# Probabilities divided on GpSimd, mixed values kept on chip

## The reference

```
proj = rmsnorm(x) @ w_in
oa = window attention  (8 query heads, 2 key heads, rotary, keys within 128, a sink per head)
ob = neighbourhood attention (8 heads, grid of 64 columns, 8 rows x 16 columns, bias table)
    s = q k * scale (+ bias or mask);  p = exp(s - max);  o = (p / sum p) v
x  = x + concat(rmsnorm(oa, g_out_a), rmsnorm(ob, g_out_b)) @ w_out
h  = rmsnorm(x);  aff = softmax(h @ w_router);  each of 16 experts takes its best tokens
x  = x + sum over experts of gate * SwiGLU(h)
y  = rmsnorm(x, g_final)
```

## Time and profile before

| | us |
|---|---|
| median of 3 runs (2483.33 to 2484.32) | 2483.69 |
| the profiled execution | 2484.71 |
| its span in the profile | 2482.9 |

### The profile page before, as it was taken

How to read it: one execution, slowest core, us unless ns; L and a number is a source line. 1 busy time by engine, 2 the same in 40 slices (tenths; PEclk the granted TensorE clock), 3 DMA queues, 4 the chain that set the end, 5 groups by cost and what they waited for, 6 DMA issues and landing times.

```text
span 2482.9 us, 43086 instructions
## 1 busy us (share of the span) xinstructions
PE 2434.5 (98%) x16395; PEld 2178.7 (88%) x16395; DVE 1673.5 (67%) x2432; ACT 1456.5 (59%) x2050; POOL 163.7 (7%) x172
## 2 busy tenths in 40 slices
PE   9999999999889999999999999999999999999997
PEld 7888877777579989899998989999998989999896
DVE  6355278854776767676666767666676767666677
ACT  4332189977555656556565656555565655656574
POOL 0000000000010101101010100101010110101010
PEclk9999999999989999999999999999999999999998
DMA  7353255354376767767676767767676776767696
GB/s 250 123 177 113 62 163 202 122 186 154 111 286 224 260 224 258 240 241 247 234 248 233 250 234 248 256 230 251 223 259 226 256 244 238 251 230 253 228 325 222
DMA packets 104549, 545.29 MB, mean 220 GB/s; under 512 B 11344, under 2 KB 19920, under 8 KB 54800
## 3 DMA queue, kind: packets, MB, share of 16 engines
q1 hardware_dynamic: 97072, 518.19, 59.6%
q0 software_dynamic: 7392, 25.96, 4.5%
HBM read 503.21 MB, written 40.89 MB: 219 GB/s over the span
## 4 chain that ended last, share of the span: by engine, by line
PE 69%; DVE 1%; DMA 1%; ACT 1%; issue 0%; POOL 0%; SPq 0%; DVEq 0%; ACTq 0%
PE ex_gate_ps L2043 16%; PE ex_up_ps L2043 16%; PE ex_gate_ps L2045 7%; PE ex_up_ps L2045 7%; PE ex_down_ps L2058 2%; PE ex_down_ps L2062 2%; PE ex_down_ps L2059 2%; PE ex_down_ps L2060 2%; PE ex_down_ps L2063 2%; PE ex_up_ps L2058 2%; PE ex_up_ps L2062 2%; PE ex_up_ps L2063 2%; PE ex_up_ps L2060 2%; PE ex_up_ps L2059 2%; DMA fi_x<-acc_scratch 1%; PE ex_turn_ps L2011 0%
## 5 line engine op out<-in xcount | busy, mean ns | idle before, releaser
L1879 DVE TENSOR_TENSOR ex_w_lo<-ex_w,ex_w_hi 128x2048 fp32r<-128x2048 f32 x384 | 879.8, 2292 | 440.5 <-ACT ex_w_hi L1775 437.1
L1775 ACT ACTIVATE ex_w_hi<-ex_w 128x2048 fp32r<-128x2048 f32 x384 | 733.4, 1910 | 208.7 <-PE ex_down_ps L2063 106.8
L2043 PE MATMUL ex_gate_ps<-ex_xt,ex_w_hi 128*128 128x384 f32 x2048 | 591.8, 359 | 0.7 <-DVE ex_xt L1885 0.7
L2043 PE MATMUL ex_up_ps<-ex_xt,ex_w_hi 128*128 128x384 f32 x2048 | 592.1, 359 | 0.0
L2045 PE MATMUL ex_up_ps<-ex_xt,ex_w_lo 128*128 128x192 f32 x2048 | 512.7, 250 | 0.0
L2045 PE MATMUL ex_gate_ps<-ex_xt,ex_w_lo 128*128 128x192 f32 x2048 | 512.7, 250 | 0.0
L2045 PEld LDWEIGHTS ex_gate_ps<-ex_xt,ex_w_lo 128*128 128x128 f32 x2048 | 391.1, 191 | 0.6
L2045 PEld LDWEIGHTS ex_up_ps<-ex_xt,ex_w_lo 128*128 128x128 f32 x2048 | 391.2, 191 | 0.0
L2043 PEld LDWEIGHTS ex_gate_ps<-ex_xt,ex_w_hi 128*128 128x128 f32 x2048 | 384.5, 188 | 1.6 <-issue 1.0
L2043 PEld LDWEIGHTS ex_up_ps<-ex_xt,ex_w_hi 128*128 128x128 f32 x2048 | 384.5, 188 | 0.0
L1797 ACT ACTIVATE ex_up_low<-ex_up_ps 128x384 f32<-128x384 f32 x128 | 62.9, 492 | 207.8 <-PE ex_up_ps L2045 207.8
(11 more groups left out here) (310 smaller groups left out, 4012.3 us busy)
## 6 DMA issues: line engine op xcount, KB each, us to landing
ex_w<-in_w_experts SPq DMA_DIRECT2D x384, 1024.0 KB, 4.8
pj_w<-in_w_in SPq DMA_DIRECT2D x54, 512.0 KB, 3.7
pj_xr<-in_xt SPq DMA_DIRECT2D x12, 512.0 KB, 6.0
o_scratch<-ld_out SPq DMA_DIRECT2D x24, 256.0 KB, 4.6
at_bias<-in_near_bias SPq DMA_DIRECT2D x4, 1536.0 KB, 8.8
q_p<-in_x SPq DMA_DIRECT2D x12, 512.0 KB, 4.5
acc_scratch<-k_p SPq DMA_DIRECT2D x12, 512.0 KB, 5.4
h_scratch<-q_p SPq DMA_DIRECT2D x12, 512.0 KB, 3.0
```

The source lines that it names most:

```text
L1775: act.activation(w_hi[:, c % SLOTS, :], w[:, c % SLOTS, :], ACT.Copy).then_inc(hi_w, 1)
L1879: dve.tensor_tensor(w_lo[:, c % SLOTS, :], w[:, c % SLOTS, :], w_hi[:, c % SLOTS, :].bitcast(F32), ALU.subtract).then_inc(lo_w, 1)
L2043: nc.tensor.matmul(out[:, b, 0:2 * CAP], w_hi[:, slot, f], xt[:, k, :, :].rearrange("p h c -> p (h c)"), start=k == 0, stop=False)
```

## The change

In `attend` the reciprocals are taken one turn earlier (unit u-1), and GpSimd multiplies the probabilities of each head by them in place. The flips, still of unit u-2, wait for GpSimd. Values are weighed for unit u-3, and DVE copies the mixed tile of unit u-4, which is already transposed, over that unit's own queries, `queries(v)`. The two output transposes, ACT's copy for them, the multiplication on DVE and all traffic of `o` are gone. Scores have four banks, probabilities eight slots, the bias two slots, the mixed tile two banks. At the end ACT and DVE prepare the first tile and four slices of `w_out`.

In `mix` tiles are read from the queries by `Mixed.parts`, in three pieces (a 128x512 one, two strided 128x256 ones). Every tile keeps the two head groups apart (A and B) and is scaled when it is added, in two adds of two instructions each. The sums of squares are made from squares on ACT, two folding adds on GpSimd and a matmul against ones (`tally`), two tiles at a time. Rows of `w_out` and `g_out` are reordered to match on the host.

```diff
@@ attend
-        PROBS, STATS, BIASES, V_SLOTS, SCORES = 4, 8, 3, 2 * len(V_TILES), 3
+        PROBS, STATS, BIASES, V_SLOTS, SCORES = 8, 8, 2, 2 * len(V_TILES), 4
-        FLIP, WEIGH, OUT, STEPS = 2, 4, 4, N + 4
+        INVERT, FLIP, WEIGH, OUT = 1, 2, 3, 4
+        STEPS = N + OUT + 1
+        def queries(v, rows):
+            b, pair, _ = units[v]
+            if b.window:
+                return keep.q.at(rows, pair, b.tile * P, P)
+            return keep.q.at(rows, QA + pair, b.kind * GROUP + b.strip * P, P)
...
+                    if not b.window and b.number + BIASES < len(near_start):
+                        sp.wait_ge(added, 2 * PAIRS * (step + 1))
                         load_bias(b.number + BIASES)
...
+        @block.gpsimd
+        def _(pool):
+            for v in range(N):
+                b, r = units[v][0], v % STATS
+                pool.wait_ge(inverted, v + 1)
+                for h in range(2):
+                    p = probs[:, (2 * v + h) % PROBS, 0:b.keys]
+                    pool.tensor_scalar(p, p, rden[:, r, h:h + 1], None, ALU.mult).then_inc(shared_out, 1)
@@ scalar
-                    act.activation(o_turn[:, v % 2, :], mixed_ps[:, 0:P], ACT.Copy).then_inc(o_copied, 1)
...
                 if u == N - 1:
-                    split(0)
+                    act.wait_ge(kept, PAIRS * (FIRST_TILES + 1))
+                    for dst, src in mixed.parts(0, lead.m_hi):
+                        act.activation(dst, src, ACT.Copy).then_inc(lead.hi_m, 1)
+                if N <= u < N + LEAD_SPLITS:
+                    split(u - N)
@@ vector
+                if 0 <= u - OUT < N:
+                    v = u - OUT
+                    dve.wait_ge(weighed, v + 1)
+                    dve.tensor_copy(queries(v, slice(0, P)), mixed_ps[v % 2][:, 0:P]).then_inc(kept, 1)
@@ tensor
-                        pe.wait_ge(exped, 2 * v + h + 1)
+                        pe.wait_ge(shared_out, 2 * v + h + 1)
...
-                    turned = [nc.tensor.transpose(out_ps[:, h, 0:HD], o_turn[ROWS[h], v % 2, :],
-                                                  ident[ROWS[h], ROWS[h]]) for h in range(2)]
@@ mix, gpsimd
+            for t in range(TILES):
+                own = squares[:, t % 2, :, :].rearrange("p (l j) c -> p l j c", l=2)
+                pool.wait_ge(mixed_squared, Mixed.PARTS * (t + 1))
+                pool.tensor_tensor(own[:, :, 0:2, :], own[:, :, 0:2, :], own[:, :, 2:4, :], ALU.add).then_inc(paired, 1)
...
+                pool.tensor_tensor(partial[:, t % (2 * PAIR), :, :], own[:, :, 0, :], own[:, :, 1, :],
+                                   ALU.add).then_inc(folded, 1)
@@ mix, scalar: before the steps, then at the end of each
+            for t in range(2):
+                square_mixed(t)
+            for j in range(LEAD_SPLITS, DT):
                 split(j)
             raise_m(1)
+            take_root1(0)
...
+                if s + 3 < TILES:
+                    square_mixed(s + 3)
@@ mix, vector
+                    dve.scalar_tensor_tensor(out=x2[t % 2][:, c], in0=bank_of(t, part, k)[:],
+                                             scalar=rs1[:, i % 2, col:col + 1],
+                                             in1=(x if part == A else x2)[t % 2][:, c],
+                                             op0=ALU.mult, op1=ALU.add).then_inc(summed, 1)
...
+                add(t, B)
...
+                if s % 2 == 0 and s < TILES:
+                    invert1(s // 2)
...
+                if t < LAST:
+                    scale_h(t)
+                    search(s, 1)
+                    if n < TILES:
+                        lower(n)
+                    add(s, A)
+                dve.wait_ge(routed, t + 1)
@@ mix, tensor
+            def tally(i):
+                pe.wait_ge(folded, PAIR * (i + 1))
+                for t in range(PAIR * i, PAIR * (i + 1)):
+                    for part in (A, B):
+                        col = 2 * (t % PAIR) + part
+                        last = nc.tensor.matmul(ss1[:, col:col + 1], partial[:, t % (2 * PAIR), part, :], ones[:],
+                                                start=True, stop=True)
+                last.then_inc(tallied, 1)
...
-                    if n < TILES:
-                        turn_merged(n)
```

More of the change, by code:

```diff
@@ L114 @@
 class Lead:
[L118 to L123, removed]
-        self.m_hi, self.m_lo = sb("ld_m_hi", [P, DT, P], F32R)[:], sb("ld_m_lo", [P, DT, P], F32R)[:]
[L125 to L135, removed]
+    FIRST_LO, HI = 6, 4
@@ L136, in __init__, with parts @@
         self.w_in = [sem(f"ld_w_in{i}") for i in range(DT)]
-        self.squared, self.root, self.refined = sem("ld_squared"), sem("ld_root"), sem("ld_refined")
-        self.normed, self.turned = sem("ld_normed"), sem("ld_turned")
         self.hi_m, self.lo_m, self.hi_w, self.lo_w = (sem(f"ld_{n}") for n in ("hi_m", "lo_m", "hi_w", "lo_w"))
[L140 to L150, removed]
+class Mixed:
+    PARTS = 1 + 2
+    def __init__(self, q):
+        self.q = q
+    def parts(self, t, dst):
+        rows, tile = slice(0, P), self.q.at(slice(0, P), slice(0, QA), t * P, P)
+        pieces = [(dst[:, 0:QA, :], tile)]
+        g, first = divmod(t, G_TILES)
+        strips = self.q.at(rows, slice(QA, DT), g * GROUP, GROUP).rearrange(
+            "p j (s r c) -> p j s r c", s=STRIPS, r=Q_ROWS)
+        into = dst[:, QA:DT, :].rearrange("p j (r s c) -> p j r s c", r=2, s=STRIPS)
+        return pieces + [(into[:, :, r, :, :], strips[:, :, :, 2 * first + r, :]) for r in range(2)]
@@ new lines, in square_mixed, with take_root1 @@
+            def square_mixed(t):
+                if t >= 2:
+                    act.wait_ge(folded, t - 1)
+                for dst, src in mixed.parts(t, squares[:, t % 2, :, :]):
+                    act.activation(dst, src, ACT.Square).then_inc(mixed_squared, 1)
+            def take_root1(i):
+                act.wait_ge(tallied, i + 1)
+                if i:
+                    act.wait_ge(refined1, REFINE * i)
+                act.activation(rt1[:], ss1, ACT.Sqrt, bias=eps[:], scale=1.0 / HALF).then_inc(root1, 1)
@@ L1407, in _ @@
                     last.then_inc(parted, 1)
-                both(s, range(3, 5))
+                if s < TILES:
+                    project(s, B, pieces[3:5])
+                if s == 0:
+                    pe.wait_ge(ready, 1)
+                    tally(0)
                 if 0 <= t:
@@ L2226, in layouts @@
     a["sink"] = np.broadcast_to(i["sink_a"][0][order], (P, 2 * PAIRS))
-    a["w_out"] = i["w_out"][0].reshape(DT, P, D)
+    mixed = [HD * h + e for h in order for e in range(HD)] + list(range(D // 2, D))
+    a["w_out"] = i["w_out"][0][mixed].reshape(DT, P, D)
     router = i["w_router"][0].reshape(DT, P, EXPERTS).transpose(1, 0, 2)
```

507 lines of the change are left out of this document (198 added, 309 removed).

## The result

The changed kernel takes 2560.68 us (median of 4 runs, 2560.18 to 2562.11) against 2484.01 in the runs beside it: slower by 3.1%, ratio 1.0310, 95% interval 1.0292 to 1.0328. The profiled execution's span went from 2482.9 to 2558.5 us. The forecast was 2474 with a range to 2495.

A forecast was written before the change was run, and what follows sets the result against it. TensorE was taken to set attention's turn (PE busy 185.0 of 185.9 us). Attention -13.3, bias +1.0, seam +0.7, steady steps +0.7 and search steps +0.6 sum to -10.3: 2483.7 to 2473.4, stated as 2474 us, range 2466 to 2495.

The forecast's parts named there:

- step 3: Attention: two bias slots instead of three make a stall for the last block's bias, +1.0 us (0 to 4).
- Step 1: Attention: TensorE loses two output transposes and gets back 0.21 us a turn, 2.08 to 1.87 us at 384 keys.
- Step 2, the ring: Attention: flips wait for GpSimd, which waits for DVE's reciprocal; two turns of 384 keys take 2.45+2X us.
- the price: Attention: X, the time of one GpSimd multiplication, is 0.63 us for 384 columns, between 0.49 and 1.01.
- Step 4: Between attention and mixing: extra copies and splits make the passage 41.4 us against 40.7, +0.7 us (0 to +2.5).
- Step 5: Mixing, steady steps: DVE's half add makes TensorE wait 0.9 us, not 0.42; seven steps, +0.7 us (-3.5 to +2).
- Step 6: Mixing steps under DVE's search: half add and scaled add bring 1.5 us, passing one step by 0.6; +0.6 us.
- A: Attention: GpSimd dearer than a turn can carry, breaking even at 0.83 us an instruction; 2495 to 2504 us; chance 0.22.
- TensorE's clock: Attention: sign of wrong working if the granted clock falls below 1.00 because of TensorE's new waits; no size given.

The follow-up runs named there:

- experiment 5: Changed kernel with GpSimd multiplying only 138 of 384 columns (the forecast's price), the rest left undivided: 2509.19 us, ratio 1.0105.
- experiment 6: Changed kernel with GpSimd multiplying only 138 of 384 columns and the flips three turns behind the scores, not two: 2483.64 us, ratio 0.9998.
- experiment 3: Changed kernel with flips three turns behind the scores, not two, mixing and keeping one turn later, GpSimd's work unchanged: 2514.52 us.
- experiment 9: Kernel before the change with only its two output transposes a turn left out, the output staying unturned: 2479.26 us, ratio 0.9981.
- experiment 12: Changed kernel with GpSimd copying each head's probabilities onto themselves in place of multiplying them: 2495.47 us, ratio 1.0039.
- experiment 10: Changed kernel with GpSimd's multiplication left out altogether, flips waiting for the exponentials: 2483.58 us, ratio 0.9999.
- experiment 7: Changed kernel with DVE's half add in the mixing stage moved behind the routing probabilities: 2561.26 us.

## Why the prediction was wrong, point by point

The forecast's 2474 and the measured 2560.7 differ by 86.7 us, which the runs split: price 51.5 (2560.7 to experiment 5's 2509.2), ring 25.6 (to experiment 6's 2483.6), the rest 9.6. The first two depend on the order in which they are mended: with the ring opened first (experiment 3) the ring is worth 46.2 and the price 30.9. Of the rest 6.9 are attention (in experiment 6 the last exponential came 6.4 us sooner than before, not 13.3) and 3.0 the seam, where the longer pipeline took 3.7 more than before and not 0.7; the bias wait that did not come (step 3) gives 1.0 back.

- **Step 1 (0.21 us a turn back from TensorE): failed by its size.** It is 0.05 (experiment 9). Forecast 20 us with nothing in the way, 4.5 measured. The number was read as a distance between two starts in the earlier trace rows.
- **Step 2, the ring (2T=2.45+2X): failed.** It followed the chain from ACT's copy of the flips to the exponentials and let DVE take the reciprocal 0.06 us behind them. In the order of DVE's loop the reciprocal stands behind the bias additions of the next unit, whose scores stand on TensorE behind the flips and the mixing. The reciprocal of before stands in just that place (401.99 in the earlier trace rows, right behind an addition); nobody waited for it there. The ring measured is 2X+3.43.
- **Step 2, the price (X=0.63 between 0.49 and 1.01): failed.** 1.25 for 384 columns, above the upper bound. The bound took the *slope* of a two-operand multiplication, 2.19 ns, with the *fixed part* of a one-column copy. The measured slope is (1252-764)/192 = 2.5 ns and the fixed part 0.28 us. "One operand read stands between none and two" is what experiment 12 refutes: a copy reads one operand and costs 0.88 ns a column like the memset; and a tile times a scalar is dearer than a tile times a tile: 1.25 us for 384 columns, by its slope about 1.58 for 512 (an estimate), beside 1.29 for 512.
- **Step 3 (bias slots +1.0): not seen.** No wait for a bias is in the trace, nor in that of experiment 10 at full pace.
- **Step 4 (seam +0.7, up to 2.5): +2.06.** Step 0 began 8.8 us after the last exponential (577.51), forecast 9.2. The price of blocking that the prediction named is in the trace: two splits on DVE took 4.01 us beside GpSimd's folding, where one takes 1.27 alone, and GpSimd's own fold 1.61, not 0.73. From the start of step 0 to the transposes of step 1 it is then 19.95 us (577.51 to 597.46), forecast 12.6+5.8=18.4, and in it TensorE waits twice for DVE's late slices, 0.28 and 0.67 us (last row for the longer). That the folding is the cause of the whole extra 1.4 us was not tried by itself.

```profile
580.08 0.73 POOL L1103 TENSOR_TENSOR mx_partial<-mx_squares 128x256 f32<-128x256 f32 x1
580.77 1.29 POOL L1099 TENSOR_TENSOR mx_squares<-mx_squares 128x512 f32<-128x512 f32 x1
580.82 4.01 DVE L1199 SCALAR_TENSOR_TENSOR ld_w_lo<-ld_w,gain_out,mx_w_hi 128x1024 fp32r<-128x1024 f32 x2 [3.75 <-ACT mx_w_hi L1123]
582.14 1.61 POOL L1103 TENSOR_TENSOR mx_partial<-mx_squares 128x256 f32<-128x256 f32 x1
584.75 1.27 DVE L1199 SCALAR_TENSOR_TENSOR ld_w_late<-v_s,gain_out,mx_w_hi 128x1024 fp32r<-128x1024 f32 x1
...
587.27 0.19 PEld L194 LDWEIGHTS mx_ps<-mx_w_hi,ld_m_hi 128*128 128x128 f32 x1 [0.67 <-DVE ld_w_late L1199]
```

- **Step 5 (steady steps 13.7 to 13.8): right in size, partly by luck.** They alternate, 13.90 and 13.54, and only the mean, 13.72 against 13.68, is as forecast. The two kinds of step have two causes, of which the prediction saw one. Where the tally of squares runs it fills the wait and costs more than the wait (13.90); where it does not, the half add makes TensorE wait 0.68 us (this row, beside the last of the earlier trace rows); experiment 7 takes 0.26 of that away.

```profile
618.38 0.09 PEld L1358 LDWEIGHTS mx_ps<-ident,mx_aff 128*16 128x16 f32 x1 [0.68 <-DVE mx_aff L1274]
```

- **Step 6 (step 10 above 14, +0.6): right.** 14.21 us, +0.52.
- **The rivals.** A was the right direction (GpSimd dearer than a turn can carry) with a decision point, X=0.83, that was itself worked out from the wrong ring. By 2X+3.43 a wide turn of 2.08 would need X of 0.37, which is under both of the prediction's bounds. The ring could have been walked in the trace of before: half of the flips 0.27 (of the 0.53 from their start to the mixing), mixing to scores 0.80 and, on DVE's timeline there, scores (402.05) to the first addition 0.95, from it to the reciprocal 0.96, and the prediction's own 0.16+0.10 to GpSimd. That is 3.24 in all, and a wide turn above the old 2.08 at every price inside the bounds (2.11 at 0.49):

```profile
403.00 0.56 DVE L863 CUSTOM_DVE_ANT_0 at_raw<-at_score,at_bias 128x384 f32<-128x384 f32 x1 [0.20 <-PE at_score L922]
...
403.96 0.16 DVE L870 RECIPROCAL at_rden<-at_sums 128x2 f32<-128x2 f32 x1
```

- **The rule that spoke against the edit.** The trace shows one multiplied operand at 2.5 ns a column and a copy at 0.88. The GPSIMD Engine Reference of the Trainium skill (section 4.1) says that elementwise arithmetic belongs on VectorE, two inputs being about twice slower on GpSimd and one input roughly at line rate. The runs bear the advice out as far as GpSimd's division costs 77 us (experiment 10); line rate fits the copy here, but not the multiplication, and there the measurement decides. The page's best case of 1.8 cycles an element (section 3.1; an estimate of 1.5 ns a column) lies below the measured slope and gave no bound for this instruction.
- **TensorE's clock: the sign came, but it is a small part.** The prediction named a granted clock below the 1.00 of the earlier trace rows as a sign of being wrong, and it was 0.98 in attention. In two stretches it stood at the lower of its two levels (0.50, 1.2 GHz), for about 6.8 us from 319.3 on and 3.4 from 472.9 on; for the rest it stood at the higher (1.00, 2.4 GHz). Before the first of them TensorE had waited 1.26 and 0.57 us for GpSimd. That the new waits bring it about is not shown: experiment 9, which has none of them, has 3.4 us at the lower level at the start of attention too. What it costs, two traces with the same attention tell: with 6.8 us less of it, experiment 7 goes from the first scores to the last exponential in 252.5 us and the changed kernel in 254.0. All of it would be some 2 of the 72 us (an estimate from these two). Rows of the changed kernel:

```profile
319.40:326.00 6.60, 6.45 (x46) 4.33 (x48) 3.42 (x14) 4.00 (x14) 3.90 (x5) 0.50 0.41 133
326.50:472.50 146.00, 115.56 (x1408) 76.78 (x1406) 95.66 (x383) 84.59 (x270) 120.08 (x111) 1.00 0.28 93
473.00:476.00 3.00, 3.00 (x22) 1.85 (x20) 1.00 (x3) 1.39 (x6) 1.25 (x2) 0.50 0.02 5
```

## What to carry to other kernels

Before an edit adds a link between engines, walk the whole ring in *program order* of every engine on it: an instruction that nobody waited for so far (here the reciprocal) starts where its list lets it, and what stands ahead of it becomes part of the path. Price a removed instruction by what its neighbour was ready to do without it, not by the distance between two starts. And where an operation has no row, do not scale the nearest one down and call it the upper bound: here the whole 1.29 us of the 512-column multiplication would only just have covered the 1.25. Ask whether the edit survives at the lower bound too.

## What the runs showed of the hardware

- GpSimd's tensor-by-scalar multiplication of fp32: 2.5 ns a column and 0.28 us fixed through a pointer (0.20 with a constant), the same slope from 96 to 384 columns; its copy 0.88 ns a column and 0.17 us fixed (0.29 us for 128 columns written from two broadcast elements, 0.51 for 384).
- GpSimd's multiplications beside DVE's attention work did not stretch: the maximum, 1252 ns, is the usual value at 384 columns. Beside DVE's 128x1024 splits both engines' instructions did, as shown at step 4.
- DVE's reciprocal costs by the column: 0.16 us for 2, 0.94 for 128.
- Two 64-row transposes between the flips and the mixing cost TensorE 0.05 us a turn (experiment 9) although their matmuls show 0.23 us of busy time.
